# Two-block transformer kernel in split fp32: part of the low-order halves made by accumulating DMA transfers

## The reference

```python
D_MODEL, SEQ = 1024, 512
D_FF = 2816            # 22 chunks of 128

def swiglu(x, w_gu, w_down):
    g, u = jnp.split(x @ w_gu, 2, axis=-1)
    return (jax.nn.silu(g) * u) @ w_down
```

## Time and profile before

| | us |
|---|---|
| median of 3 runs | 2214.07 (2213.58 to 2215.66) |
| the profiled execution | 2213.68 |
| its span, first to last instruction | 2211.8 |

### The profile page before, as it was taken

The page is one execution under the profiler, slowest core; times in us unless marked ns, Lnnn a source line. Parts: engine busy times, 40 slices in busy tenths (PEclk is TensorE's granted clock), DMA queues, the critical chain, the costliest instruction groups (busy, mean ns, idle before and its releaser), DMA issues.

```text
span 2211.8 us, 33448 instructions
## 1 busy us (share of the span) xinstructions
PE 2147.3 (97%) x12698; PEld 1836.8 (83%) x12698; DVE 1460.8 (66%) x2344; ACT 1082.7 (49%) x1700; POOL 320.9 (15%) x267
## 2 busy tenths in 40 slices
PE   9999999998999999999999999999999999999998
PEld 6788887788999978877889989878778778888887
DVE  6766666479999843455689999556666665555522
ACT  5445555345454544565444555355565554444312
POOL 0221222310000030002200000300111144222211
PEclk9999999999999999999999999999999999999999
DMA  3311111221222322201213222331221222222221
GB/s 140 115 58 39 58 39 39 74 91 65 96 96 96 125 92 89 79 36 39 96 65 107 96 96 100 130 132 58 72 72 39 72 97 96 98 101 102 96 95 57
DMA packets 31675, 185.00 MB, mean 84 GB/s; under 512 B 3104, under 2 KB 7712, under 8 KB 11312
## 3 DMA queue, kind: packets, MB, share of 16 engines
q1 hardware_dynamic: 29520, 175.48, 22.9%
q0 software_dynamic: 2016, 7.60, 1.0%
HBM read 178.84 MB, written 7.37 MB: 84 GB/s over the span
## 4 chain that ended last, share of the span: by engine, by line
PE 74%; DVE 13%; ACT 5%; issue 4%; DMA 2%; SPq 0%; DVEq 0%; POOL 0%; ACTq 0%; POOLq 0%
PE ps L2331 20%; PE ps L2333 19%; PE ps L2332 19%; DVE wl L1483 3%; DMA raw<-in_stream 2%; PE ps L2657 2%; PE ps L3148 1%; ACT wh L525 1%; PE ps L3091 1%; PE ps L3131 1%; PE ps L2651 1%; DVE wsum L1454 1%; ACT wh L657 1%; PE ps L3158 1%; PE ps L2923 1%
## 5 line engine op out<-in xcount | busy, mean ns | idle before, releaser
L2331 PE MATMUL ps<-xh,wh 128*128 128x512 f32 (+1 forms) x1616 | 610.3, 378 | 13.3 <-DVE act_up L1380 9.4
L2333 PE MATMUL ps<-xh,wl 128*128 128x512 f32 (+1 forms) x1616 | 584.0, 361 | 0.0
L2332 PE MATMUL ps<-xl,wh 128*128 128x512 f32 (+1 forms) x1616 | 582.8, 361 | 0.0
L2331 PEld LDWEIGHTS ps<-xh,wh 128*128 128x128 f32 x1616 | 306.0, 189 | 63.4 <-issue 12.1
L2333 PEld LDWEIGHTS ps<-xh,wl 128*128 128x128 f32 x1616 | 305.1, 189 | 48.0
L2332 PEld LDWEIGHTS ps<-xl,wh 128*128 128x128 f32 x1616 | 306.0, 189 | 42.4 <-issue 4.3
L1229 DVE TENSOR_TENSOR wl<-raw,wh 128x2048 fp32r<-128x2048 f32 x92 | 212.8, 2313 | 175.7 <-ACT wh L525 175.6
L525 ACT ACTIVATE wh<-raw 128x2048 fp32r<-128x2048 f32 x92 | 175.9, 1912 | 161.1 <-PE ps L2333 160.8
L2331 PE MATMUL ps<-part_h,wh 128*128 128x256 f32 (+1 forms) x672 | 221.7, 330 | 6.0 <-DVE hT L1520 3.9
L2333 PE MATMUL ps<-part_h,wl 128*128 128x256 f32 (+1 forms) x672 | 220.3, 328 | 0.0
L2332 PE MATMUL ps<-part_l,wh 128*128 128x256 f32 (+1 forms) x672 | 219.8, 327 | 0.0
(11 more groups left out here) (427 smaller groups left out, 4069.0 us busy)
## 6 DMA issues: line engine op xcount, KB each, us to landing
raw<-in_stream SPq DMA_DIRECT2D x158, 1024.0 KB, 4.8
hankd<-tabd SPq DMA_DIRECT2D x1, 3072.0 KB, 17.3
hank<-hankd POOLq DMA_DIRECT2D x4, 768.0 KB, 5.1
hT<-in_xT SPq DMA_DIRECT2D x4, 512.0 KB, 6.1
keepd<-hT POOLq DMA_DIRECT2D x1, 2048.0 KB, 10.1
hT<-keepd POOLq DMA_DIRECT2D x8, 256.0 KB, 4.8
out<-hT SPq DMA_DIRECT2D x8, 256.0 KB, 2.5
raw<-in_stream SPq DMA_DIRECT2D x2, 512.0 KB, 7.7
```

Of the source, the lines that this page charges most:

```text
L2331: pe.matmul(out, w_hi, a_hi, start=start, stop=False, skip_group_check=goes_on)
L2332: pe.matmul(out, w_hi, a_lo, start=False, stop=False, skip_group_check=goes_on)
L2333: return pe.matmul(out, w_lo, a_hi, start=False, stop=stop, skip_group_check=goes_on)
```

## The change

Of each unit's seven pieces, two (k = 1 and k = 6, `ADDED_BY_DMA`) no longer get their rest from DVE. ACT rounds the quarter into `wh` and then writes the same quarter once more, negated and rounded, into `wl`. POOL waits for that and issues a transfer (`weight_rest`) that reads the quarter of 256 KB again from the DRAM `stream` and adds it to `wl` in place (`accum_op=ALU.add`): the quarter minus its rounded part. The PE waits for the landing of that transfer. The same is done for two of the four rests of a pair, those of `ssq` and `sq` (`pair_rests`, source and destination both in SBUF); `pair_sums` of the next pair waits for both landings.

ACT takes the two kinds in another order: pieces with k = 1 or 6 are rounded at step p for piece p+6, the others still for p+5 (`rounded_in`, `HIGHS`). The raw slot is now released by piece k = 5 of a unit (`hi_made`, `lo_made`), one piece before k = 6. Three existing semaphores (`h_back[0..2]`) count the landings. The core of the diff:

```diff
+ADDED_BY_DMA = (1, 6)
...
-SPLITS = running(lambda j, k: k != 6)
+DONE = running(lambda j, k: k != 6)
+RESTS = running(lambda j, k: k in (0, 2, 4, 3))
...
+def rounded_in(p):
+    if p == -2:
+        return ORDER[:LEAD]
+    at = [(p + SUM_LEAD, True), (p + HI_LEAD, False)]
+    return [ORDER[i] for i, by_dma in at if LEAD <= i < len(ORDER) and (ORDER[i][1] in ADDED_BY_DMA) == by_dma]
+ROUNDED = [q for p in range(-2, len(ORDER)) for q in rounded_in(p)]
+HIGHS = {q: sum(k != 5 for _, k in ROUNDED[:i + 1]) for i, q in enumerate(ROUNDED)}
...
-        each = {part_hi: SPLITS[last_piece] + 3, part_lo: SPLITS[last_piece] + 3, prod_done: SPLITS[last_piece],
+        highs, rests = len(ORDER) - len(STREAM), RESTS[last_piece]
+        rest_added = {1: h_back[0], 6: h_back[1]}
+        each = {part_hi: highs + 3, part_lo: rests + 3, prod_done: DONE[last_piece],
...
+        pair_rest_added = h_back[2]
+        def pair_rests_by_dma(f, pairs):
+            return pair_rest_added, 32 * (REST // 2 * f + pairs)
+        def rest_by_dma(f, j, k):
+            return rest_added[k], 16 * (len(STREAM) * f + j + 1)
...
-                    act.activation(part_h[:, 3 * i + 1, :], ssq[:, :], ACT.Copy).then_inc(hid_hi_made, 1)
-                    act.activation(part_h[:, 3 * i + 2, :], sq[:, :], ACT.Copy).then_inc(hid_hi_made, 1)
+                    act.activation(part_h[:, 3 * i + 1, :], ssq[:, :], ACT.Copy)
+                    act.activation(part_l[:, 3 * i + 1, :], ssq[:, :], ACT.Copy, scale=-1.0).then_inc(hid_hi_made, 1)
+                    act.activation(part_h[:, 3 * i + 2, :], sq[:, :], ACT.Copy)
+                    act.activation(part_l[:, 3 * i + 2, :], sq[:, :], ACT.Copy, scale=-1.0).then_inc(hid_hi_made, 1)
...
-                    act.activation(wh[:, half, w], source_of(f, j, k), ACT.Copy).then_inc(hi_made if k == 6 else part_hi, 1)
+                    if k in ADDED_BY_DMA:
+                        act.activation(wh[:, half, w], source_of(f, j, k), ACT.Copy)
+                        act.activation(wl[:, half, w], source_of(f, j, k), ACT.Copy, scale=-1.0).then_inc(part_hi, 1)
+                    else:
+                        act.activation(wh[:, half, w], source_of(f, j, k), ACT.Copy).then_inc(hi_made if k == 5 else part_hi, 1)
...
-                        if p + HI_LEAD < len(ORDER):
-                            hi(*ORDER[p + HI_LEAD])
-                        elif p + HI_LEAD < len(ORDER) + 4:
+                        for q in rounded_in(p):
+                            hi(*q)
...
+                        dve.wait_ge(*pair_rests_by_dma(f, m))
...
-                    dve.tensor_tensor(xl[:, i, TOK:], act_of(2 * m)[:, 0:TOK], xh[:, i, TOK:].bitcast(F32), ALU.subtract)
-                    dve.tensor_tensor(part_l[:, 3 * i, :], act_of(2 * m + 1), part_h[:, 3 * i, :].bitcast(F32), ALU.subtract)
-                    dve.tensor_tensor(part_l[:, 3 * i + 1, :], ssq[:, :], part_h[:, 3 * i + 1, :].bitcast(F32), ALU.subtract).then_inc(hid_lo_made, 1)
-                    dve.tensor_tensor(part_l[:, 3 * i + 2, :], sq[:, :], part_h[:, 3 * i + 2, :].bitcast(F32), ALU.subtract).then_inc(hid_lo_made, 1)
+                    dve.tensor_tensor(xl[:, i, TOK:], act_of(2 * m)[:, 0:TOK], xh[:, i, TOK:].bitcast(F32), ALU.subtract).then_inc(hid_lo_made, 1)
+                    dve.tensor_tensor(part_l[:, 3 * i, :], act_of(2 * m + 1), part_h[:, 3 * i, :].bitcast(F32), ALU.subtract).then_inc(hid_lo_made, 1)
...
-                    dve.wait_ge(part_lo, fast_count(part_lo, f, SPLITS[j, 1]))
+                    dve.wait_ge(part_hi, fast_count(part_hi, f, HIGHS[j, 1]))
...
-                    if k == 6:
+                    if k == 5:
...
-                        if p + LEAD < len(ORDER):
+                        if p + LEAD < len(ORDER) and ORDER[p + LEAD][1] not in ADDED_BY_DMA:
...
+            def weight_rest(f, j, k):
+                half, w = weights_of(f, j, k)
+                q = {1: 1, 6: 3}[k]
+                landed, n = rest_by_dma(f, j, k)
+                pool.wait_ge(part_hi, fast_count(part_hi, f, HIGHS[j, k]))
+                if n > 16:
+                    pool.wait_ge(landed, n - 16)
+                pool.dma_start(wl[:, half, w], io["stream"][stream_unit(FAST[f], j)][:, SEQ * q:SEQ * q + SEQ], accum_op=ALU.add).then_inc(landed, 16)
+            def pair_rests(f, m):
+                landed, n = pair_rests_by_dma(f, m)
+                if n:
+                    pool.wait_ge(landed, n)
+                for i, sums in ((1, ssq), (2, sq)):
+                    pool.wait_ge(hid_hi_made, FC * f + 2 * m + i)
+                    pool.dma_start(part_l[:, 3 * (m % 4) + i, :], sums[:, :], accum_op=ALU.add).then_inc(landed, 16)
+            def rests(f):
+                pair_rests(f, 0)
+                for p in range(-2, len(ORDER)):
+                    for j, k in rounded_in(p):
+                        if k in ADDED_BY_DMA:
+                            weight_rest(f, j, k)
+                    if p - 1 in PAIR_SUMS_AT:
+                        pair_rests(f, PAIR_SUMS_AT[p - 1])
             sum_squares("ffn0")
+            rests(0)
             sum_squares("kv")
             for c in range(6):
                 fill_lo_chunk("sb_out", c, om_sb)
             sum_squares("ffn1")
+            rests(1)
...
-                        pe.wait_ge(part_hi, fast_count(part_hi, f, SPLITS[j, k]))
-                        pe.wait_ge(part_lo, fast_count(part_lo, f, SPLITS[j, k]))
+                        pe.wait_ge(part_hi, fast_count(part_hi, f, HIGHS[j, k]))
+                        pe.wait_ge(*(rest_by_dma(f, j, k) if k in ADDED_BY_DMA else (part_lo, fast_count(part_lo, f, RESTS[j, k]))))
...
+                        pe.wait_ge(*pair_rests_by_dma(f, n + 4))
```

More of the change, by code:

```diff
@@ L441, in piece_done @@
                 return units_used, stream_unit(FAST[f], j) + 1
-            return prod_done, fast_count(prod_done, f, SPLITS[j, k])
+            return prod_done, fast_count(prod_done, f, DONE[j, k])
+        pair_rest_added = h_back[2]
[3 more added lines that the diff above has]
+            return rest_added[k], 16 * (len(STREAM) * f + j + 1)
         def slot_free(f, j, k):
@@ L666, in copy_out @@
                 def copy_out(j, k):
-                    act.wait_ge(prod_done, fast_count(prod_done, f, SPLITS[j, k]))
+                    act.wait_ge(*piece_done(f, j, k))
                     last = gate_before(j)
@@ L701, in ffn_fast @@
                 gate_up(4)
-                for p in ORDER[:LEAD]:
-                    hi(*p)
+                for q in rounded_in(-2):
+                    hi(*q)
                 gate_up(5)
-                hi(*ORDER[LEAD])
+                for q in rounded_in(-1):
+                    hi(*q)
                 products()
@@ L1281, in split_out @@
                     if name == "mix_out":
-                        dve.wait_ge(h_back[c], 16)
+                        dve.wait_ge(h_back[c], 16 * (2 * len(STREAM) if c < 2 else 2 * REST if c == 2 else 0) + 16)
                     if c < 3:
@@ L1449, in first_sums @@
                     if j:
-                        dve.wait_ge(part_lo, fast_count(part_lo, f, SPLITS[j - 1, 4]))
+                        dve.wait_ge(part_lo, fast_count(part_lo, f, RESTS[j - 1, 4]))
                         dve.wait_ge(weights_summed, fast_count(weights_summed, f, 4 * j))
@@ L1478, in lo @@
                     half, w = weights_of(f, j, k)
-                    if k == 6:
+                    if k == 5:
                         dve.wait_ge(hi_made, stream_unit(name, j) + 1)
                     else:
-                        dve.wait_ge(part_hi, fast_count(part_hi, f, SPLITS[j, k]))
-                    dve.tensor_tensor(wl[:, half, w], source_of(f, j, k), wh[:, half, w].bitcast(F32), ALU.subtract).then_inc(lo_made if k == 6 else part_lo, 1)
+                        dve.wait_ge(part_hi, fast_count(part_hi, f, HIGHS[j, k]))
+                    dve.tensor_tensor(wl[:, half, w], source_of(f, j, k), wh[:, half, w].bitcast(F32), ALU.subtract).then_inc(lo_made if k == 5 else part_lo, 1)
                 def down_lo(q):
@@ L1488, in down_lo @@
                     if q < 3:
-                        dve.wait_ge(part_hi, fast_count(part_hi, f, SPLITS[last_piece] + q + 1))
+                        dve.wait_ge(part_hi, fast_count(part_hi, f, highs + q + 1))
                     else:
@@ L1561, in ffn_fast @@
                 sums(*ORDER[1])
-                for p in ORDER[:LEAD]:
-                    lo(*p)
+                for j, k in ORDER[:LEAD]:
+                    if k not in ADDED_BY_DMA:
+                        lo(j, k)
                 sums(*ORDER[LEAD])
@@ L2503, in down_rest @@
                             if b in (0, 4, 8):
-                                pe.wait_ge(part_hi, fast_count(part_hi, f, SPLITS[last_piece] + b // 4 + 1))
-                                pe.wait_ge(part_lo, fast_count(part_lo, f, SPLITS[last_piece] + b // 4 + 1))
```

(2 more changed lines are left out.)

5 lines of the change are left out of this document (3 added, 2 removed).

## The result

The changed kernel takes 2267.07 us in the median (2262.94 to 2278.27, 4 runs) against 2214.86 (2213.58 to 2217.40, 4 runs): a ratio of 1.024, 95% interval 1.020 to 1.028. Predicted were 2194 us. The profiled execution took 2262.94 us.

The account below looks back on a forecast made before the run. PE, 97% busy, bounds the kernel, idling where DVE is late in gates with pairs; 23.9 us won in the rest less 3.6 lost in the head takes 2213.68 to 2193.4, predicted as 2194 us; 8-in-10 range 2182 to 2219.

Parts of the forecast that it names:

- the rest: Both stages after their first twelve pieces: PE waits of 15.1 and 13.8 us, 28.9 together, of which 23.9 would be won.
- The raw slot comes free one piece earlier: SP's 1 MB loads of `raw`: slot released 1.4 us earlier; counted at nothing by itself, as it lies beside PE work.
- ACT's 29.8 us: ACT's waits for landings of `raw`: most would go, to under 10 us in a stage.
- The additions' own landing: POOL's 256 KB accumulating transfers: 5 us each, covered by PE work, no gain or cost; showing above 6 us.
- Rival A: Accumulating transfers are slow and the PE pays piece by piece: level at 6.5 to 7 us, 2230 at 8; chance 0.20.
- The head: First twelve pieces of each stage: `pair_sums(2)` waits for pair 1's landing until 527.4; 1.8 us lost a stage.
- ACT's order: Negations delay `pair_lo` and `gated`: 0.5 us lost for each of four later pairs, 2.5 us a stage staying in all.
- Rival B: Transfers in time, but ACT and longer `pair_hi` become late: 7 us won, 2207 us (2203 to 2214); chance 0.16.
- the forecast's 20.3 us: Net gain over both stages: 23.9 us won behind the first twelve pieces less 3.6 lost in them.

Follow-up runs that it names:

- e10: Against e8, each addition covers only 16 of 512 columns (part of the computation left out): 2186.5 us, ratio 0.987 to before.
- e3: Changed kernel with ACT rounding k = 5 ahead of k = 6 in each step, SP waiting for both: 2232.8 us, 1.009 of before.
- e8: Against e3, DVE also starts `pair_lo` about 1.04 us earlier, when `ssq`'s copies are made: 2225.4 us, 1.006 of before.
- e13: Full change, k = 6 rounded seven pieces ahead instead of six, `pair_lo` begun as in e8: 2223.2 us, 1.004 of before.
- e14: Against e13, all pairs' rests back on DVE, 48 additions a stage: 2207.8 us, 0.997 of before.
- e1_short: Changed kernel, same waits, copies and issues, but each addition moves 16 of 512 columns (part of the computation left out): 2205.8 us, 0.996 of before.
- e6: Changed kernel with only k = 1 by addition (24 a stage), k = 6 and all pairs on DVE: 2271.6 us, 1.026 of before.
- e2: Changed kernel with the same full-size transfers as plain copies, not additions (part of the computation left out): 2212.5 us, 0.999 of before.
- e15: Against e7, its one addition a unit, k = 6, is rounded seven pieces ahead (24 a stage, pairs on DVE): 2198.1 us, 0.992 of before.
- e7: Changed kernel with only k = 6 by addition, k = 5 rounded first, k = 1 and pairs on DVE: 2218.7 us, 1.002 of before.

## Why the prediction was wrong

**What bounded the kernel before: half right.** The PE's waits and DVE's load were read rightly: e10 takes away all but 2.3 of the rest's 15.1 us. What was missed is the second loop right beside it. The load's own period was never worked out; it was 9.6 us in downs and 10.2 in the last gates against 9.97, and SP's starts in the trace of before show it.

**"The raw slot comes free one piece earlier": right as a step (4.8 to 3.2 us), wrong in its result.** It said that most of ACT's 29.8 us goes, with the landing taken as fixed at 4.8 us. This is the step that failed: ACT's wait rose to 45.1 us, because the landing rose to 7.7 us with the additions beside it, and 7.7 + 3.2 is more than 9.97. The prediction weighed what a load does to the additions ("beside a load of 1 MB whose DMA share is about 0.3") and not what the additions do to the load.

**The additions' own landing: mis-sized, and taken as one.** 5 us was taken, between 3.1 and 11.3; measured were 4.4 us for k = 6 and 8.2 for k = 1. Time was counted for k = 6 (7.8 us free, "for k = 1 it is more"); the PE was ready for k = 1 8.3 us after the issue in the median, 5.0 in the worst unit, so k = 1, held to be the safe one, is where the PE waits: 11.8 us of its gaps. Rival A put the point of balance at 6.5 to 7 us and 2230 at 8 us, and had the sign. Its mechanism holds for e3, e8 and e13, where 12 to 15 us remain before the added pieces while ACT waits 8 to 16 us for loads. It can't be the whole in the change: e14 and e13, with k = 1's additions as slow as ever, have rests of 10.3 and 17.5 us.

**The head: right place, too small.** Predicted 1.8 us, measured 5.9 and 5.4. Chain of waits of the changed kernel there, then its PE after the last stop (timeline; in brackets the idle time before).

```profile
523.20 7.52 DMA part_l<-sq
...
530.84 0.42 DVE ssq L1429
```

```profile
538.46 0.55 PE L2393 MATMUL ps<-t_h,wh 128*128 128x256 f32 x1 [3.33 <-ACT fork L704]
...
541.16 0.41 PE L2393 MATMUL ps<-xh,wh 128*128 128x256 f32 x1
```

`pair_sums(2)` began at 530.8 and not at 527.4, since the pair's second addition, issued 0.8 us behind the first, landed after 7.5 us, beside two others and a load. And a price that wasn't in the sum: after two stops of the PE in 529 to 539, of 2.2 and 3.3 us, it ran its matmuls 0.21 us apart instead of 0.119 until 544.2. The granted clock of 530 to 540 and of 540 to 550 is 0.86 and 0.80: in part of both stretches the lower of its two levels, 1.2 GHz, was granted. In 540 to 550 the rows touch 71 matmuls, in e1_short, with a granted clock of 1.00 there, 87: 1.9 us.

**ACT's order: right mechanism, mis-sized.** The prediction gave each later pair 0.5 us of loss and kept 2.5 us of the rest for all. In e1, where only order and copies of the change act, the rest is 10.5 us, and 10.0 of it lie where the four pairs among gates run: 2.5 us in the pieces 12 to 28 (one pair), 2.7 in 56 to 84 (one; the pair at step 57, right behind the downs, costs 0.2) and 4.8 in 84 to 112 (two). That is 2.5 us a pair, 1.0 of which stands before a k = 0 in the kernel before, too. The trace shows the wait foretold for `pair_lo`:

```profile
669.35 0.42 ACT L659 ACTIVATE xh<-act_up 128x256 fp32r<-128x256 f32 x1 [1.56 <-DVE sq L1434]
...
671.75 0.61 ACT L664 ACTIVATE part_l<-sq 128x512 fp32r<-128x512 f32 x1
...
672.40 0.43 DVE L1439 TENSOR_TENSOR xl<-act_up,xh 128x256 fp32r<-128x256 f32 x1 [1.55 <-ACT part_l L664]
```

These are ACT's and DVE's timelines of the changed kernel: 1.55 us of idle DVE where there was none. Rival B was this; its 2207 us are e1's 2205.8 to a microsecond, in part by luck, since B took 7.5 us a stage for pairs and 3.5 for the head, and e1 shows 10.0 and 0.9. So with costless transfers B and not the forecast would have come out. With the order mended (e10) the forecast's 20.3 us are passed: 28.7 were won.

**The account.** First stage: 261.1, less 4.6 that the relief wins in the rest under the change's order (e1), plus 0.9 of head by order, makes 257.4. Then come the bytes: 5.0 us more of head (29.7 - 24.7) and 20.9 of rest, 283.3. These 20.9 us are the late loads and k = 1's slow additions together; e13 keeps 12.2 us of gaps before k = 1 with the loop mostly out of the way (ACT waits 8.4 us for loads there), so how they divide in the change itself stays open. The second stage lost 5.5 us more (27.7 against 22.2), and its account was not made. The range failed because it ended at 2219, short of rival A's own 2230 at 8 us, and because no rival let the new transfers slow an old one.

## What to carry to other kernels

Before transfers are added, work out the period of each loop that already contains one, landing plus the work behind it, and compare it with the pace of the bound engine; a loop 4% below the pace (9.6 us against 9.97 here) was the next bound, and new traffic beside it lengthened it even where, as in e6, the PE waited for none of the new transfers. Shorten the work between a landing and the next load (here: what stands ahead of it in ACT's order) before adding traffic. Then move as little as the relief needs and give it lead: seven pieces ahead 24 additions a stage won 17 us and 48 won 7, where 64 at six pieces lost 52. And look at which of two transfers is issued first.

## What the hardware showed that was not expected

- An accumulating transfer of 256 KB took 1.7 times a plain copy's share of the DMA engines per MB (2.9% and 1.7%, e2 beside the change) and landed after 6.5 us instead of 4.1 in the median of both kinds, at best 4.3. The 1 MB load beside them went from 4.8 to 7.7 us; beside the same number of copies, to 5.3.
- The same traffic in another order let the load land after 5.6 us (e3). One addition 2.2 us ahead of a load made it 2.3 us longer (7.1 against 4.8, e15); 3.6 us ahead it cost nothing; 0.1 us behind, the addition itself took 6.5 us instead of 4.3 (e7). When transfers are issued matters as much as how many. How two that start within 1 us share the engines stays open, and a run with the traffic alone, without the change's dependences, was not made.
- DVE's sum of two SBUF tensors took 1.27 us instead of 0.69 while POOL subtracted, and POOL's subtraction 1.52 us.
